# Sums of the modulation pieces on TensorE, placed ahead of the turns of a head's output

## The chip, the cores and the metric

The kernel runs on one core of one Trainium2 chip. The time is the device time of one execution, in microseconds (us); where several executions are given, their median counts.

## What is computed

A trunk of two layers, 1024 tokens by 1024 features, in f32. Layer 0 mixes by attention, layer 1 by gated linear attention; each is followed by a SwiGLU FFN. Every sub-layer is shifted, scaled and gated by a conditioning vector `c`, and that *modulation* is what the change is about. Cut to what matters:

```python
def reference(x, c, ada_w, ada_b, ...):
    for l in range(DEPTH):
        mod = (jax.nn.silu(c) @ ada_w[l] + ada_b[l])[:, None, :]
        sh1, sc1, g1, sh2, sc2, g2 = jnp.split(mod, 6, axis=-1)
        h = rmsnorm(x, norm_g[l, 0]) * (1 + sc1) + sh1
        ...   # mixer: layer 0 has 4 differential heads (A) and 8 dilated heads (B)
        x = x + (1 + g1) * rmsnorm(y, norm_g[l, 1])
        h = rmsnorm(x, norm_g[l, 2]) * (1 + sc2) + sh2
        y = swiglu(h, ffn_w_gate[l], ffn_w_up[l], ffn_w_down[l])
        x = x + (1 + g2) * rmsnorm(y, norm_g[l, 3])
    return x
```

## The kernel before

TensorE (PE) carries the matmuls, and its instructions run in the order in which they are written. Layer 0's attention is a loop over eight blocks, `attention_block(kind, b, slot, last)`. Blocks 0 to 3 are the four A heads (kind 0), blocks 4 to 7 are four pairs of B heads (kind 1). Within a block PE goes over eight rows n of 128 queries:

- `scores(n, b, slot)` (line 936) multiplies queries by keys; VectorE (DVE) adds the bias and takes the maximum (line 2094), which also frees the score banks. `scores(n + 1)` may start only when row n has been read.
- `turn_weights(n)` (line 957) transposes the softmax weights, and `weigh(n)` (line 970) multiplies them by V.
- `chunk(c)` (lines 822, 823 and 826) is a piece of the next block's input projection: 24 matmuls of 512 columns.

At the end of block b stands a seam, which is where the change is. PE runs `turn_v(b + 1)` (line 922, the next block's V), `scores(0, b + 1)`, and then `turn_out()` (line 982): eight transposes of the block's output `o_sb`, four into bank 4 and four into bank 5. They wait for the output: in kind 0 for DVE's scaling of `o_sb` (line 2153, signalled by the drain at 2155), in kind 1 for ScalarE's (ACT) last copy into it (line 1500). The banks must be free too: DVE copies the next V out of bank 5 at line 2071. After the turns ACT reads each bank into `y_st_hi` (line 1543), DVE subtracts that to get `y_st_lo` (line 2163 in kind 0, 2166 in kind 1), and only then does DVE go on to the next block's row 0 (line 2094), which `scores(1)` of the next block waits for.

The modulation is worked out in pieces beside this. In block b (0 to 6) DVE adds up eight weight rows times `silu(c)` into `acc_one` (part of `rinv`, lines 2052 and 2054). `ada_sum(b)` (lines 906 to 913) then sums over the 128 partitions on PE, with two matmuls by a tile of ones into banks 1 and 3. The trace shows each f32 matmul as two records, so there are four records at line 912. DVE's `columns` (line 2003) reads the result in row 1 of the next block; `scores(4)` waits for that through `mod_done`. `ada_sum(b)` is called after `attention_block` returns, so it stands behind the turns.

Below, seam b is the stretch from `scores(0, b + 1)` to the first chunk of block b + 1. Seam 6 has no chunk behind it.

Of the kernel before, what the change touches and what calls it, by code (L numbers as in the profile page):

```python
# [51 lines left out]
def trunk_kernel(nc, xT, cT, weights, ada_w, ada_bT, norm_gT, lam_p, subln_g, w_g2, b_g2, head_g,  # L52
# [5 lines left out]
    with ctx:  # L58
# [47 lines left out]
        def bank(b, n=512):  # L106
            return ps[:, b * 512:b * 512 + n]
# [260 lines left out]
        def lanes(kind, n):  # L368

            if kind == 0:  # L370
                if n < 4:
                    return [(0, n % 2, 0, n + 1)]
                return [(0, 0, 0, 4), (0, 1, 4, n - 3)]
            out = []
            for k0 in range(0, n + 1, 4):
                for c in (0, 1):
                    out.append((c, c, k0, min(4, n + 1 - k0)))
            return out

        def lane_count(kind, n, lane):  # L380

            return 1 + sum(g[1] == lane for m in range(n) for g in lanes(kind, m))

        def events(b, t):
            return LANE[0] * min(b, 4) + LANE[1] * max(b - 4, 0) + t
# [419 lines left out]
        def _(pe):  # L805
# [23 lines left out]
            def chunk(c):  # L829

                u, half = chunk_of(c)
                if c > 1:
                    before = c - 2 if c < 7 else c - 1
                    if before % 6 < 4:
                        pe.wait_ge(qk_lo, qk_count(before))
                    else:
                        pe.wait_ge(v_out, v_count(before))
                unit(u, u % 2, chunk_bank(c), half if c in (0, 2) else None, hh[half], hl[half], done=ch_done)
# [67 lines left out]
            def ada_sum(b):  # L906

                pe.wait_ge(acc_done, b + 2)
                pe.wait_ge(s_read[0], 8 * b + 9)
                pe.wait_ge(s_read[1], 8 * b + 9)  # L910
                for i in range(2):
                    mm = pe.matmul(bank(1 + 2 * i), ones[:, :], acc_one[:, i * 512:(i + 1) * 512], start=True, stop=True)
                mm.then_inc(ada_mm, 1)

            def turn_v(b, group):
                pe.wait_ge(v_out, 2 * b + 2)
                for lane in range(2):

                    pe.wait_ge((ta_free, td_free)[lane], group)
                    for n in range(4):  # L920
                        m = 4 * lane + n
                        mm = pe.transpose(bank(4 + lane)[:, n * P:(n + 1) * P], v_sb[:, m * P:(m + 1) * P], ident[:, :])
                    mm.then_inc((ta_done, td_done)[lane], 1)

            def scores(n, b, slot):
                pe.wait_ge(s_read[0], 8 * b + n + 1)
                pe.wait_ge(s_read[1], 8 * b + n + 1)
                if n == 0:
                    pe.wait_ge(qk_lo, 4 * b + 4)
                W = 256 * ((n + 2) // 2)  # L930
                for k0 in range(0, W, 512):
                    w = min(512, W - k0)
                    for term, (q, k) in enumerate(((q_high, k_high), (q_low, k_high), (q_high, k_low))):
                        for c in range(2):
                            rows = slice(64 * c, 64 * c + 64)
                            mm = pe.matmul(ps[:, c * 1024 + k0:c * 1024 + k0 + w],  # L936
                                           q[slot][rows, n * P:(n + 1) * P], k[slot][rows, k0:k0 + w],
                                           start=term == 0, stop=term == 2)
                            if term == 2 and k0 + w == W:
                                mm.then_inc(s_done[c], 1)  # L940

            def attention_block(kind, b, slot, last=False):
                before = lambda t: events(b, t)

                def turn_weights(n, part=0):

                    count = [lane_count(kind, n, lane) + part for lane in range(2)]
                    if kind == 0:
                        pe.wait_ge(w_done, 8 * b + n + 1 + 1)
                    for c, lane, k0, m in lanes(kind, n):  # L950
                        if kind == 1 and k0 != 4 * part:
                            continue
                        if kind == 1:
                            pe.wait_ge(exp_done, 16 * b + 2 * n + c + 1 + 1)
                        pe.wait_ge((ta_free, td_free)[lane], before(count[lane]) + 1)
                        for i in range(m):
                            mm = pe.transpose(bank(4 + lane)[:, i * P:(i + 1) * P],  # L957
                                              pr[n % 2][:, c, (k0 + i) * P:(k0 + i + 1) * P], ident[:, :])
                        mm.then_inc((ta_done, td_done)[lane], 1)
                        count[lane] += 1  # L960

                def weigh(n):

                    pe.wait_ge(ta_free, before(lane_count(kind, n + 1, 0)) + 1)
                    pe.wait_ge(td_free, before(lane_count(kind, n + 1, 1)) + 1)
                    pe.wait_ge(o_done, 8 * b + n + 1)
                    for c in range(1 if kind == 0 else 2):
                        for kb in range(n + 1):

                            mm = pe.matmul(bank(6)[:, c * P:(c + 1) * P], wT[n % 2][c][:, kb, :],  # L970
                                           v_tok[:, kb, :], start=kb == 0, stop=kb == n)
                    mm.then_inc(pv_done, 1)

                def turn_out():
                    if kind == 0:
                        pe.wait_ge(o_ready, b + 1)
                    else:
                        pe.wait_ge(o_done, 8 * b + 8 + 1)
                    for lane in range(2):
                        pe.wait_ge((ta_free, td_free)[lane], before(LANE[kind] + (not last)))  # L980
                        for n in range(4):
                            mm = pe.transpose(bank(4 + lane)[:, n * P:(n + 1) * P], o_sb[:, 4 * lane + n, :], ident[:, :])
                        mm.then_inc((ta_done, td_done)[lane], 1)

                scores(1, b, slot)
                for n in range(8):
                    if kind == 1:
                        turn_weights(n)
                        if n:
                            weigh(n - 1)  # L990
                    if n == 2 and b:
                        pe.wait_ge(mod_done, b + 1)
                    if n < 6:
                        scores(n + 2, b, slot)
                    if kind == 0:
                        turn_weights(n)
                        if n:
                            weigh(n - 1)
                    elif n > 3:
                        turn_weights(n, 1)  # L1000
                    if n < 6 and not last:
                        chunk(6 * (b + 1) + n)
                        if (b, n) == (6, 5):
                            pe.drain().then_inc(unit_used, 24)
                weigh(7)
                if not last:
                    turn_v(b + 1, before(LANE[kind]))
                    scores(0, b + 1, 1 - slot)
                turn_out()

            def attention():

                for c in range(6):
                    chunk(c)
                turn_v(0, 1)
                scores(0, 0, 0)
                for b in range(HEADS):
                    attention_block(b // 4, b, b % 2, b == HEADS - 1)
                    if b < 7:
                        ada_sum(b)  # L1020
                pe.wait_ge(ta_free, 4 * sum(LANE) + 1)
                pe.wait_ge(td_free, 4 * sum(LANE) + 1)

# [1432 lines left out]
```

## Time and profile before

| | |
|---|---|
| time, median of 3 executions | 2680.44 us (2679.87 to 2685.88) |
| time of the profiled execution | 2687.1 us |
| its span | 2685.2 us |
| PE busy | 2541.0 us, 95% of the span |
| DVE, ACT, POOL busy | 51%, 40%, 43% |
| the 28 records of line 912 | 592 ns at the least, 593 ns median, 1062 ns at the most |
| the 64 records of line 982 | 272 ns at the least, 273 ns median, 477 ns at the most |

A row of a timeline gives the start in us from the span's start, the time from the first start to the last end, the engine, the line, the operation with its output and inputs, the count, and in brackets how long the engine had been idle before it and who ended that. Matmuls overlap, so the time of one record is more than its distance to the next.

### The profile page before, as it was taken

Reading aid. Unit: us, or ns where it says so; the run is one execution under the profiler, and the core shown is the slowest. Engines: PE = TensorE matmul, PEld = TensorE weight load, DVE = VectorE, ACT = ScalarE, POOL = GpSimd, SP = SyncE. Lnnn points to the kernel's source line nnn. Section 1 sums busy time; section 2 is a strip of 40 time slices with the busy share of each in tenths; the row PEclk is TensorE's granted clock in tenths of the full one; section 3 lists DMA queues with packets and bytes.
Section 4 is the critical chain, followed back from the end, with each engine's and each line's share of the span. In section 5 each row is a group of like instructions: output and inputs, shape, how many; then the busy total and the mean of one; then the engine's idle time right before and its main releaser. Section 6 shows DMA issues by size and latency. Waiting matters only on the chain.

```text
span 2685.2 us, 33902 instructions
## 1 busy us (share of the span) xinstructions
PE 2541.0 (95%) x12152; PEld 2073.0 (77%) x12152; DVE 1356.1 (51%) x1877; ACT 1078.5 (40%) x1837; POOL 1147.7 (43%) x648
## 2 busy tenths in 40 slices
PE   5999999998999999999999999997999999999996
PEld 3777777777778888788887777886878888788885
DVE  7466665442464333455356536667366332355145
ACT  3344543343454332334233236656454333234222
POOL 0111111011656777444444434443556777544443
PEclk8999999999999999999999999999999999999998
DMA  6233332224233122342434741223223221343333
GB/s 262 64 106 106 111 103 86 89 92 174 93 108 106 67 91 79 133 141 94 160 122 171 264 146 65 68 71 117 86 99 114 79 91 67 106 142 119 111 133 109
DMA packets 106886, 305.14 MB, mean 114 GB/s; under 512 B 11456, under 2 KB 11776, under 8 KB 106752
## 3 DMA queue, kind: packets, MB, share of 16 engines
q1 hardware_dynamic: 106752, 303.40, 32.9%
q8 instruction: 79, 1.29, 0.2%
q14 instruction: 55, 0.45, 0.1%
HBM read 262.46 MB, written 40.89 MB: 113 GB/s over the span
## 4 chain that ended last, share of the span: by engine, by line
PE 61%; issue 17%; POOL 7%; DVE 6%; ACT 3%; DVEq 2%; DMA 2%; POOLq 2%; SPq 1%; ACTq 0%
PE ps L822 8%; PE ps L826 8%; PE ps L823 8%; PE ps L1190 5%; PE ps L1186 5%; PE ps L1187 5%; POOL w_lo L696 5%; PE ps L970 3%; PE ps L1217 3%; PE ps L1220 3%; PE ps L1214 3%; PE ps L936 2%; PE ps L1039 2%; PE ps L957 2%; DVEq L2223 2%
## 5 line engine op out<-in xcount | busy, mean ns | idle before, releaser
L696 POOL TENSOR_TENSOR w_lo<-w_raw,w_hi 128x1024 fp32r<-128x1024 f32 x258 | 632.0, 2452 | 1344.3 <-ACT w_hi L1285 585.4
L822 PE MATMUL ps<-h_hi,w_hi 128*128 128x512 f32 x1288 | 521.7, 405 | 21.4 <-DVE h_lo L1827 8.4
L823 PE MATMUL ps<-h_lo,w_hi 128*128 128x512 f32 x1288 | 510.2, 396 | 0.0
L1285 ACT ACTIVATE w_hi<-w_raw 128x1024 fp32r<-128x1024 f32 x178 | 188.3, 1058 | 448.5 <-PE ps L1220 293.6
L826 PE MATMUL ps<-h_hi,w_lo 128*128 128x512 f32 x1288 | 319.6, 390 | 0.0
L1895 DVE TENSOR_TENSOR a_lo<-arena,a_hi 128x512 fp32r<-128x512 f32 x88 | 206.8, 2350 | 221.7 <-ACT a_hi L1752 221.7
L822 PEld LDWEIGHTS ps<-h_hi,w_hi 128*128 128x128 f32 x1288 | 246.8, 192 | 89.6 <-DVE h_lo L1827 15.1
L823 PEld LDWEIGHTS ps<-h_lo,w_hi 128*128 128x128 f32 x1288 | 247.1, 192 | 52.1 <-issue 2.4
L826 PEld LDWEIGHTS ps<-h_hi,w_lo 128*128 128x128 f32 x1288 | 243.1, 189 | 50.9
L1186 PE MATMUL ps<-comb,w_hi 128*128 128x512 f32 x560 | 217.8, 389 | 0.0
L1187 PE MATMUL ps<-comb,w_hi 128*128 128x512 f32 x560 | 217.8, 389 | 0.0
L745 POOL TENSOR_TENSOR w_lo<-a_f,w_hi 128x512 fp32r<-128x512 f32 x112 | 144.5, 1293 | 79.0 <-ACT w_hi L1379 79.0
L1214 PE MATMUL ps<-a_hi,w_hi 128*128 128x512 f32 x672 | 168.3, 391 | 7.9 <-issue 6.8
L1217 PE MATMUL ps<-a_lo,w_hi 128*128 128x512 f32 x672 | 168.5, 393 | 0.0
L1220 PE MATMUL ps<-a_hi,w_lo 128*128 128x512 f32 x672 | 166.7, 390 | 0.0
L1379 ACT ACTIVATE w_hi<-a_f 128x512 fp32r<-128x512 f32 x112 | 70.8, 632 | 230.3 <-PE ps L1190 83.2
L1214 PEld LDWEIGHTS ps<-a_hi,w_hi 128*128 128x128 f32 x672 | 126.0, 188 | 36.6 <-issue 8.5
L1190 PE MATMUL ps<-comb,w_lo 128*128 128x512 f32 x560 | 149.7, 389 | 0.0
L1217 PEld LDWEIGHTS ps<-a_lo,w_hi 128*128 128x128 f32 x672 | 128.1, 191 | 26.8
L1220 PEld LDWEIGHTS ps<-a_hi,w_lo 128*128 128x128 f32 x672 | 126.8, 189 | 26.5
L1485 ACT ACTIVATE pr_flat<-pr_flat,small 128x256 f32<-128x256 f32 (+7 forms) x128 | 98.3, 769 | 108.3 <-DVE small L2099 108.3
L1190 PEld LDWEIGHTS ps<-comb,w_lo 128*128 128x128 f32 x560 | 105.1, 188 | 21.8
(263 smaller groups left out, 4230.2 us busy)
## 6 DMA issues: line engine op xcount, KB each, us to landing
w_raw<-weights SPq DMA_DIRECT2D x286, 512.0 KB, 3.6
arena<-ada_w SPq DMA_DIRECT2D x80, 512.0 KB, 3.6
arena<-act_d SPq DMA_DIRECT2D x72, 256.0 KB, 3.7
act_d<-ybuf SPq DMA_DIRECT2D x56, 256.0 KB, 2.2
arena<-ada_w SPq DMA_DIRECT2D x8, 1024.0 KB, 14.8
x<-xT SPq DMA_DIRECT2D x4, 2048.0 KB, 13.3
glr<-weights SPq DMA_DIRECT2D x14, 512.0 KB, 3.6
rinv<-weights SPq DMA_DIRECT2D x28, 256.0 KB, 4.2
```

The costliest lines, as they stand in the source:

```text
L696: pool.tensor_tensor(w_lo[:, s, :], w_raw[:, s, :], w_hi[:, s, :].bitcast(f32), ALU.subtract).then_inc(lo_done, 1)
L822: pe.matmul(bank(b), w, high[:, k, :], start=k == 0, stop=False)
L823: pe.matmul(bank(b), w, low[:, k, :], start=False, stop=False)
L826: mm = pe.matmul(bank(b), w_lo[:, s, k * P:(k + 1) * P], high[:, k, :], start=False, stop=k == KB - 1)
L1186: pe.matmul(bank(b), w, high[:, k, :], start=k == 0, stop=False)
L1187: pe.matmul(bank(b), w, low[:, k, :], start=False, stop=False)
L1190: mm = pe.matmul(bank(b), combo_part(w_lo, q)[:, k * P:(k + 1) * P], high[:, k, :], start=False, stop=k == KB // 2 - 1)
L1214: pe.matmul(bank(m), w_hi[:, slot, cols[m]], a_hi[:, s, :], start=first, stop=False)
L1217: pe.matmul(bank(m), w_hi[:, slot, cols[m]], a_lo[:, s, :], start=False, stop=False)
L1220: mm = pe.matmul(bank(m), w_lo[:, slot, cols[m]], a_hi[:, s, :], start=False, stop=False)
L1285: a.activation(w_hi[:, slot, :], w_raw[:, slot, :], ACT.Copy).then_inc(hi_done, 1)
L1895: v.tensor_tensor(a_lo[:, u % 2, :], act_source(half, u), a_hi[:, u % 2, :].bitcast(f32), ALU.subtract)\
```

## The change

`ada_sum(b)` moves from behind the block to ahead of `turn_out()`. Its two matmuls and its three waits are the same.

```diff
@@ attention_block
                 if not last:
                     turn_v(b + 1, before(LANE[kind]))
                     scores(0, b + 1, 1 - slot)
+                if b < 7:
+                    ada_sum(b)
                 turn_out()
@@ attention
                 for b in range(HEADS):
                     attention_block(b // 4, b, b % 2, b == HEADS - 1)
-                    if b < 7:
-                        ada_sum(b)
                 pe.wait_ge(ta_free, 4 * sum(LANE) + 1)
```

PE at seam 0, where the turns wait for DVE. `arena` is V on its way to being turned, `qk_flat` the queries and keys, `rinv` holds the sums, and `glr` is `o_sb`. A count covers matmuls, not records:

```order
 L922 MATMUL ps<-ident,arena 128x128 x8
 L936 MATMUL ps<-qk_flat_61 128x256 x6
+L912 MATMUL ps<-rinv,ones 128x512 x2
 L982 MATMUL ps<-ident,glr 128x128 x8
-L912 MATMUL ps<-rinv,ones 128x512 x2
 L936 MATMUL ps<-qk_flat_61 128x256 x6
 L936 MATMUL ps<-qk_flat_61 128x512 x6
```

The two sums went from behind the eight turns to ahead of them, directly after the next block's row 0 scores.

PE at seam 5, between two kind 1 blocks. `pr_flat` holds the softmax weights:

```order
 L922 MATMUL ps<-ident,arena 128x128 x8
 L936 MATMUL ps<-qk_flat_60 128x256 x6
+L912 MATMUL ps<-rinv,ones 128x512 x2
 L982 MATMUL ps<-ident,glr 128x128 x8
-L912 MATMUL ps<-rinv,ones 128x512 x2
 L936 MATMUL ps<-qk_flat_60 128x256 x6
 L957 MATMUL ps<-ident,pr_flat 128x128 x2
```

The same exchange; the row 1 scores now follow the turns directly. All seven seams change alike, and the orders of DVE, ACT, POOL and SP stay as they are.

## Rows read from the trace of the kernel before

**Rows 1.** The page, busy time: us, share of the span, instructions of each engine.
```profile
PE 2541.0 (95%) x12152; PEld 2073.0 (77%) x12152; DVE 1356.1 (51%) x1877; ACT 1078.5 (40%) x1837; POOL 1147.7 (43%) x648
```

**Rows 2.** PE's longest waits, 100 to 360 us, then 360 to 600 us.
```profile
PE ps L982 <- DVEq L2155: 6.7, 4, 2.0
...
PE ps L957 <- ACT wt_flat L1479: 5.4, 7, 1.2
```

**Rows 3.** Timeline of PE at seam 0.
```profile
158.07 0.61 PE L936 MATMUL ps<-qk_flat 64*128 64x256 f32 x6
160.27 0.66 PE L982 MATMUL ps<-ident,glr 128*128 128x128 f32 x4 [1.58 <-DVEq L2155]
161.12 0.66 PE L982 MATMUL ps<-ident,glr 128*128 128x128 f32 x4 [0.19 <-DVE arena L2071]
161.61 3.56 PE L912 MATMUL ps<-rinv,ones 128*128 128x512 f32 x4
165.11 0.62 PE L936 MATMUL ps<-qk_flat 64*128 64x256 f32 x6
```

**Rows 4.** Timeline of DVE at seam 0.
```profile
163.80 0.29 DVE L2094 CUSTOM_DVE_ANT_0 pr_flat<-ps,arena 128x128 f32<-128x128 f32 x1
```

**Rows 5.** Timeline of PE at seam 2.
```profile
292.29 0.66 PE L982 MATMUL ps<-ident,glr 128*128 128x128 f32 x4 [1.58 <-DVEq L2155]
...
296.27 0.62 PE L936 MATMUL ps<-qk_flat 64*128 64x256 f32 x6 [0.75 <-DVE small L2094]
297.97 1.47 PE L936 MATMUL ps<-qk_flat 64*128 64x512 f32 x6 [1.08 <-DVE small L2094]
...
299.50 0.78 PE L822 MATMUL ps<-h_hi,w_hi 128*128 128x512 f32 x1
...
301.71 0.39 PE L823 MATMUL ps<-h_lo,w_hi 128*128 128x512 f32 x1
```

**Rows 6.** Timeline of PE at seam 1, then at seam 3.
```profile
226.67 1.97 PE L982 MATMUL ps<-ident,glr 128*128 128x128 f32 x8 [1.95 <-DVEq L2155]
...
231.11 0.62 PE L936 MATMUL ps<-qk_flat 64*128 64x256 f32 x6
...
358.86 0.66 PE L982 MATMUL ps<-ident,glr 128*128 128x128 f32 x4 [1.59 <-DVEq L2155]
...
363.64 0.63 PE L936 MATMUL ps<-qk_flat 64*128 64x256 f32 x6
```

**Rows 7.** Timeline of PE at seam 5.
```profile
512.73 0.62 PE L936 MATMUL ps<-qk_flat 64*128 64x256 f32 x6
513.28 1.09 PE L982 MATMUL ps<-ident,glr 128*128 128x128 f32 x8
514.20 1.88 PE L912 MATMUL ps<-rinv,ones 128*128 128x512 f32 x4
516.91 0.62 PE L936 MATMUL ps<-qk_flat 64*128 64x256 f32 x6 [0.82 <-DVE small L2094]
...
519.50 0.50 PE L822 MATMUL ps<-h_hi,w_hi 128*128 128x512 f32 x1
...
521.92 0.39 PE L822 MATMUL ps<-h_hi,w_hi 128*128 128x512 f32 x1
```

**Rows 8.** Timeline of PE at seam 4: a chunk's first and eleventh matmul.
```profile
441.31 0.61 PE L822 MATMUL ps<-h_hi,w_hi 128*128 128x512 f32 x1
...
445.28 0.39 PE L822 MATMUL ps<-h_hi,w_hi 128*128 128x512 f32 x1
```

**Rows 9.** Stretches at seams 0, 2, 5, 6; us, busy us (records) by engine, granted clock, DMA, GB/s.
```profile
161.67:165.08 3.41, 3.41 (x5) 0.91 (x4) 2.21 (x7) 2.64 (x5) 0.00 (x0) 0.50 0.27 107
298.20:301.61 3.41, 3.41 (x12) 2.33 (x11) 2.65 (x10) 1.54 (x6) 0.00 (x0) 0.50 1.00 338
...
513.00:522.00 9.00, 7.75 (x43) 4.97 (x42) 6.62 (x29) 4.09 (x15) 0.00 (x0) 1.00 0.57 199
595.16:601.99 6.83, 6.33 (x28) 5.21 (x28) 5.96 (x32) 3.25 (x13) 0.00 (x0) 0.50 0.73 241
```

## The prediction, made before the changed kernel was run

> **What bounds the kernel now.** I read the page's busy times first. TensorE is busy for 95% of the span [rows 1], so the time changes only where something on TensorE's own path changes. The waits of TensorE in the attention stage come next. Its longest is the one that the change aims at: the turns of an A head's output wait for DVE's scaling, 6.7 us over four seams [rows 2]. In the second stretch the longest wait is for ACT, and no wait for a DMA comes before it in that list. So a seam that ends later is not caught up by a transfer that was late anyway: I take a delay of the seam as a delay of the kernel.
>
> Then I read the seams one by one. Three things are to be seen.
>
> (a) The sums take little when the clock is full. At seam 5 the four records take 1.88 us from first start to last end and one takes 0.59 us (the least in the table above), so they start (1.88 - 0.59) / 3 = 0.43 us apart and hold TensorE for 4 x 0.43 = 1.72 us [rows 7].
>
> (b) Behind the turns a second gap opens, and the sums stand in it. After the turns ACT and DVE must read both banks, and DVE must read row 0 of the next block, before the next scores may start. At seam 5 the sums ran in that gap and TensorE still sat idle for 0.82 us [rows 7]; at seam 2 it sat idle for 0.75 us [rows 5]. There the sums cost nothing today.
>
> (c) The granted clock drops to 0.50, the 1.2 GHz level, for stretches of 3.41 us near the seams, after TensorE has had pauses, and what lies in such a stretch takes twice as long. At seam 0 it fell on the sums: 3.56 us [rows 3, 9]. At seam 2 it fell on the scores and on the first matmuls of the chunk [rows 5, 9]. At seam 5 there was none from 513 to 522 us [rows 9]. At seam 6 it was 6.83 us long [rows 9].
>
> **The change, part by part.**
>
> *Seams 0 to 3 at full clock: nothing.* The scores of row 0 start at 158.07 and hold TensorE for 0.55 us (512.73 to 513.28 with no idle time between [rows 7]). The sums then run from 158.62 to 160.34, and the first turns start 0.07 us later than today's 160.27 [rows 3]. The second four turns wait for DVE's copy until 161.12 in either order [rows 3], and it is these that the path goes through. The wait of 1.6 us is filled, but what was taken out behind the turns was hidden, so the next scores start when DVE has read row 0, as they do at seam 2. Sum: 0.
>
> *Seams 4 to 6 at full clock: a loss.* At seam 5 the turns follow the scores with no wait [rows 7]. Put ahead of them, the sums hold them back by the whole 1.72 us. Behind the turns are queued ACT's reads, DVE's low parts, row 0 on DVE and then the next scores; all of that was waited for today, as the idle 0.82 us before 516.91 shows [rows 7], and all of it moves by 1.72 us. The cover that hid the sums is left empty. Three seams: 3 x 1.72 = **+5.2 us**. This is the firmest term; only 1.72 us per seam is in play, so its bounds are 0 (some slack later in the block takes it) and 5.2.
>
> *The clock: what the low stretches cost today.* From the first turns to the next scores took 296.27 - 292.29 = 3.98 us at seam 2, at full clock [rows 5]. It took 4.84 us at seam 0 [rows 3], 4.44 at seam 1 and 4.78 at seam 3 [rows 6], so the low clock cost 0.86, 0.46 and 0.80 there. At seam 0 this agrees with DVE: its second read of row 0 starts at 163.80 [rows 4], and at seam 2 the scores start 0.45 us after that read, so here they could have started at 164.25 and not at 165.11. At seam 2 it cost 0.5 us on the scores (1.47 against about 0.95 us at full clock) and about 1.0 on the chunk: five distances between matmuls took 301.71 - 299.50 = 2.21 us [rows 5] against 5 x 0.24 = 1.21 at seam 5, where ten took 521.92 - 519.50 = 2.42 [rows 7]. Sum over seams 0 to 3: 0.86 + 0.46 + 1.5 + 0.80 = 3.6 us. At seam 4 ten distances took 3.97 us [rows 8] against 2.42, so a whole stretch on a chunk costs 1.55 us. Seam 5: none.
>
> *The clock: what they will cost.* The order of today puts 1.72 us of dense matmuls between two pauses, and at seams 0, 1 and 3 they caught much of the slow time where it is half hidden. In the new order there is one long pause from the end of the turns (161.8 at seam 0) to the scores at 164.25, then 0.6 us of work and another pause of some 1.1 us: over 4 us with little in it. I expect a low stretch behind it at every seam, on scores and chunk, where nothing hides it. One stretch costs 1.55 us there. Two in a row, as at seam 6, where waits break up the work of the first, would cost 3.1. I take the middle, 2.3, since the scores of the next rows still have waits between them when the stretch begins. Seams 0 to 3: 4 x 2.3 - 3.6 = +5.6 us (between +2.6 and +8.8). Seams 4 and 5: 2 x 2.3 - 1.55 = +3.1 us (+1.55 to +4.65). Seam 6 has two today: 0. Sum for the clock: **+8.7 us**, between +4.2 and +13.5.
>
> A rule speaks against the change too. The Trainium skill, "TensorE: Matmul & The Clock Gate", section "HAM oscillation — how this bites in real kernels", says that pauses between bursts of matmuls let the gate fall back to the slow level, so that each burst begins slow, and calls for an order of work that keeps them together. By that rule the sum is that of the clock term, about +14; without it +5.2. The trace agrees in kind: six of the seven seams show slow work, seam 5 does not.
>
> *The rest.* The three waits of the sums are met before they come: the pieces are summed by DVE in row 7, ahead of the copies that the last product needs, and the score banks were already waited for by the scores just ahead. The readers of the sums come a row later, so nobody gains by having them 2 us earlier. No other engine's order moves.
>
> *Against the profiled execution:* 2687.1 + 5.2 + 8.7 = 2701.0 us. That execution stands 6.7 us above the median of 2680.44, so on the scale of the median it is 2680.4 + 13.9 = **2694 us**.
>
> **The rivals.**
>
> *A: only the shift.* The low stretches are as many and as costly as today, and the delay at seams 4 to 6 is all: +5.2 us, 2685.6. For it: their place in the seams is different each time (on sums, on turns, on the chunk), so a new order may just deal them anew. Against it: the longer pause.
>
> *B: the sums keep the clock up, and the kernel is not slower.* In seams 0 to 3 the sums now run in the wait of 1.6 to 1.95 us ahead of the turns, so that TensorE works on without a break until the turns are done. If that pause is what sets off the low stretches, they go: 3.6 us at seams 0 to 3, 1.55 at seam 4, about 3.1 at seam 6, together -8.3, against +5.2: -3.1 us, 2677.3. It decides in favour of the change once more than 5.2 us of slow time are saved. For it: at seams 0, 1 and 3 the clock fell during or just after that wait. Against it: the gap behind the turns grows by as much as the one ahead shrinks, and seams 4 and 6 fell slow with no wait ahead of the turns.
>
> *C: nothing is passed on.* The 1.72 us at seams 4 to 6 vanish in the later rows, where TensorE waits for ACT anyway, and the clock deals as today: 0, 2680.4. Against it: ACT and DVE begin the block later by the same 1.72 us, so those waits move with it.
>
> **How the numbers follow.** About 0.3%, 8.0 us, is what a measurement of this kernel can tell from no change. Chances: forecast 0.62, A 0.27, B 0.06, C 0.05. The forecast's case runs from 5.2 + 4.2 = +9.4 to 5.2 + 13.5 = +18.7, all slower by over 0.3%; A reaches over that line now and then through a stretch dealt otherwise. Slower 0.65, same 0.33, faster 0.02. The range runs from 2684, inside A, to 2700, above the forecast's upper end of 2699.1; it leaves out B, C and the low half of A.
>
> **What would show it.** At seams 4 to 6 the turns start 1.72 us behind where they start now (513.28 + 1.72 at seam 5) and TensorE's idle time before the next scores grows from 0.8 to about 2.5 us. At seams 0 to 3 the wait of the turns for DVE falls from 1.6 us to about nothing, and an idle time of about 2.4 us appears before the next scores. The granted clock is 0.50 behind most seams, on chunk matmuls 0.43 us apart. I am wrong on the clock if the low stretches stay few, and wrong on the shift if the turns at seam 5 start where they did or if the block behind them is shorter by as much.

## The result: slower by half a per cent

| | before | changed |
|---|---|---|
| time, median | 2680.44 us (5 executions) | 2695.75 us (5 executions, 2693.41 to 2697.67) |
| ratio of the times | | 1.0053, 95% interval 1.0041 to 1.0066 |
| time of the profiled execution | 2687.1 us | 2696.83 us |
| its span | 2685.2 us | 2694.9 us |

The change costs 15.3 us by the medians and 14.2 us by the ratio, whose interval runs from 11.0 to 17.7. The forecast was 2694 us.

### The profile page after: what moved, and what is told of

It reads as the page before. It is cut to its first block, busy times and chain, and to the rows that moved or that the text cites. A ratio compares the mean times of both kernels' runs of the same rounds, so it can differ in the third digit from the quotient of the medians.

```text
span 2694.9 us, 33902 instructions
## 1 busy us (share of the span) xinstructions
PE 2542.1 (94%) x12152; PEld 2074.8 (77%) x12152; DVE 1355.2 (50%) x1877; ACT 1078.6 (40%) x1837; POOL 1148.1 (43%) x648
## 4 chain that ended last, share of the span: by engine, by line
PE 61%; issue 17%; POOL 7%; DVE 5%; ACT 3%; DVEq 2%; DMA 2%; POOLq 2%; SPq 1%; ACTq 0%
PE ps L822 8%; PE ps L826 8%; PE ps L823 8%; PE ps L1187 5%; PE ps L1190 5%; PE ps L1186 5%; POOL w_lo L696 5%; PE ps L970 3%; PE ps L1217 3%; PE ps L1220 3%; PE ps L1214 3%; PE ps L936 3%; PE ps L1039 2%; PE ps L957 2%; DVEq L2223 1%
## 5 line engine op out<-in xcount | busy, mean ns | idle before, releaser
L1187 PEld LDWEIGHTS ps<-comb,w_hi 128*128 128x128 f32 x560 | 105.1, 188 | 21.8
## 6 DMA issues: line engine op xcount, KB each, us to landing
arena<-ada_w SPq DMA_DIRECT2D x8, 1024.0 KB, 14.9
x<-xT SPq DMA_DIRECT2D x4, 2048.0 KB, 13.3
```

The source lines that it names most:

```text
L1187: pe.matmul(bank(b), w, low[:, k, :], start=False, stop=False)
```

## The profile after

The page's busy times hardly move, as the work is the same. (The columns are those of [rows 1].)

```profile
PE 2542.1 (94%) x12152; PEld 2074.8 (77%) x12152; DVE 1355.2 (50%) x1877; ACT 1078.6 (40%) x1837; POOL 1148.1 (43%) x648
```

PE's waits for DVE's reading of row 0 in the kernel before, first from 100 to 360 us and then from 360 to 600 us (us in total, times, longest):

```profile
PE ps L936 <- DVE small L2094: 4.0, 4, 1.1
...
PE ps L936 <- DVE small L2094: 3.8, 7, 0.8
```

PE's waits in the changed kernel, in the same two stretches:

```profile
PE ps L936 <- DVE small L2094: 10.6, 6, 2.5
...
PE ps L982 <- DVE arena L2071: 0.2, 1, 0.2
...
PE ps L936 <- DVE small L2094: 8.1, 5, 2.5
```

The wait that the change aimed at is gone: the 6.7 us of the turns for DVE's scaling [rows 2] have no row any more. In its place the scores wait for DVE's reading of row 0, up to 2.5 us at a time: 10.6 us where it was 4.0. In the second stretch, where no wait was removed, it is 8.1 us where it was 3.8.

The timeline of PE at seam 0 after the change shows both, and what the clock makes of it:

```profile
155.60 0.62 PE L936 MATMUL ps<-qk_flat 64*128 64x256 f32 x6
156.15 1.98 PE L912 MATMUL ps<-rinv,ones 128*128 128x512 f32 x4
157.97 1.34 PE L982 MATMUL ps<-ident,glr 128*128 128x128 f32 x8
161.79 1.01 PE L936 MATMUL ps<-qk_flat 64*128 64x256 f32 x6 [2.48 <-DVE small L2094]
163.88 1.65 PE L936 MATMUL ps<-qk_flat 64*128 64x512 f32 x6 [1.08 <-DVE small L2094]
...
172.54 0.97 PE L936 MATMUL ps<-qk_flat 64*128 64x512 f32 x6
```

It answers to [rows 3]. The sums take 1.98 us and not 3.56, the turns follow without a wait, and then PE is idle for 2.48 us. The next two groups of scores are slow (1.01 and 1.65 us, against 0.62 and 0.98 at full clock). From `scores(0)` to `scores(3)` of the next block is 16.94 us. In the kernel before it was 173.55 - 158.07 = 15.48 us, by its `scores(3)`:

```profile
173.55 0.96 PE L936 MATMUL ps<-qk_flat 64*128 64x512 f32 x6
```

Some of the stretches of low clock behind the seams of the changed kernel, at seams 0, 1, 3 and 5 (columns as in [rows 9]):

```profile
161.50:168.30 6.80, 5.43 (x20) 3.90 (x21) 4.51 (x21) 3.10 (x12) 0.00 (x0) 0.50 0.90 295
229.80:236.60 6.80, 5.75 (x21) 4.10 (x21) 4.82 (x22) 3.55 (x13) 0.00 (x0) 0.50 0.89 293
...
366.30:369.70 3.40, 3.40 (x11) 2.14 (x11) 2.48 (x11) 1.26 (x5) 0.00 (x0) 0.51 1.01 324
...
523.30:526.70 3.40, 3.40 (x11) 2.33 (x12) 2.72 (x13) 1.63 (x6) 0.00 (x0) 0.51 0.98 312
```

There is one behind each of the seams 0 to 5: 6.8 us long behind seams 0 to 2, 3.4 us behind seams 3 to 5. All of them lie on scores and chunk.

At seam 5 the shift can be read from the chain of work that ended last, which is followed back from the end of the stretch. This is a piece of it, before the change (start in us, us, what):

```profile
512.80 0.55 PE ps L936 x6
513.35 0.60 PE ps L982 x4
```

and after:

```profile
515.67 0.56 PE ps L936 x6
516.22 1.91 PE ps L912 x4
518.14 0.45 PE ps L982 x4
```

The sums were not on the chain and now they are.

From such rows comes a table of the seams. Each number is the time from `scores(0)` to `scores(3)` of the next block, in us, in one profiled execution. "Full clock" is what a seam took where the granted clock stayed at 1.00 and no added work held up its end. For seams 0 to 3 it comes from a run with the sums in both places (below); at seam 3 one run had the old order at full clock as well, and took 15.3 us too. For seams 4 and 5 it is the old order in the first experiment, and at seam 5 in the kernel before.

| seam | 0 | 1 | 2 | 3 | 4 | 5 |
|---|---|---|---|---|---|---|
| full clock | 14.6 | 15.0 | 14.6 | 15.3 | 13.3 | 13.3 |
| before | 15.5 | 15.4 | 16.0 | 16.2 | 14.9 | 13.3 |
| changed | 16.9 | 17.4 | 17.2 | 16.7 | 16.6 | 16.6 |

Seams 0 to 3 grew by 5.1 us in sum and seams 4 and 5 by 5.0. Seam 6 grew by 1.7 (9.3 to 11.0). The rows between the seams are as long as before to 0.03 us (50.55 us in blocks 1 to 3), but for one low stretch in block 5 of the kernel before (506.4 to 509.8 us), which this execution of the changed kernel does not have, and for the rows behind seam 6, which took 1.2 us more (20.1 against 18.9) with a low stretch on them. Over the attention stage, from `scores(0)` at seam 0 to 616.40 us before and 625.55 us after, that makes 11.6 us.

## The experiments

Three theories stood against each other. Theory 1 is that of the prediction: a shift at seams 4 to 6, and low stretches of the clock brought by the emptied gap behind the turns. Theory 2 is rival A, the shift alone. Theory 3 stands for the other rivals as each expectation puts it. The kernel before was timed again beside them. For the first three below and for the idle work at seams 0 to 3 its median is 2682.47 us (29 executions); for the other three it is 2681.66 us (23 executions). A difference "by the ratio" is the ratio times that median. Added lines shift the line numbers: line 936 (scores) becomes 937 or 941, line 982 (turns) 983 or 987, line 912 (sums) 917 in some, line 2094 (DVE's reading) 2096 to 2103, and line 2155 (its drain) 2164.

### The new order at seams 0 to 3 only

```diff
+                if b < 4:
+                    ada_sum(b)
                 turn_out()
+                if 4 <= b < 7:
+                    ada_sum(b)
```

> The sums ahead of the turns at seams 0 to 3 only; behind them, as before, at seams 4 to 6. Theory 1 (shift and clock): nothing at full clock, because the wait for DVE hides the sums, but low stretches move to scores and chunk: +5.6 us on the kernel before (+2.6 to +8.8), and the rows show about 2.4 us idle before the next scores. Theory 2 (shift only, low stretches dealt as before): within 1 us of the kernel before. Theory 3 (the filled wait keeps the clock up): -3.6 us.

Measured: 2687.86 us, ratio 1.0019 (1.0010 to 1.0028), +5.1 us by the ratio (2.7 to 7.5) where theory 1 said +5.6. PE at seam 0:

```profile
158.55 1.34 PE L982 MATMUL ps<-ident,glr 128*128 128x128 f32 x8
162.37 0.68 PE L936 MATMUL ps<-qk_flat 64*128 64x256 f32 x6 [2.47 <-DVE small L2096]
164.10 1.65 PE L936 MATMUL ps<-qk_flat 64*128 64x512 f32 x6 [1.05 <-DVE small L2096]
```

The wait ahead of the turns is gone and the kernel is slower. At these seams nothing is shifted: the scores of row 1 start 3.82 us after the turns, which is the 3.98 us of full clock at seam 2 before [rows 5] less the turns' own wait for the bank (0.19 us). What is lost is lost behind them, at low clock. Theories 2 and 3 fall for seams 0 to 3.

### The new order at seams 4 to 6 only

```diff
+                if 4 <= b < 7:
+                    ada_sum(b)
                 turn_out()
+                if b < 4:
+                    ada_sum(b)
```

> The sums ahead of the turns at seams 4 to 6 only; behind them at seams 0 to 3. Theory 1: the shift of 1.8 us at each of three seams, +5.5 us, and low stretches on the chunks at seams 4 and 5, +3.1 us: +8.6 us on the kernel before. Theory 2: +5.5 us. Theory 3 (absorbed later in the block): 0.

Measured: 2691.56 us, ratio 1.0036 (1.0022 to 1.0050), +9.7 us by the ratio (5.9 to 13.4). Theory 1 had said +8.6; theory 2's +5.5 lies just below the interval. The two halves add up: 5.1 + 9.7 = 14.8 us against 14.2 for the whole by the ratio and 15.3 by the medians. PE at seam 4, and the granted clock over seam 3 (old order), in seam 4 and in seam 5 (columns as in [rows 9]):

```profile
440.68 0.62 PE L936 MATMUL ps<-qk_flat 64*128 64x256 f32 x6 [2.54 <-DVE small L2096]
...
442.38 1.65 PE L936 MATMUL ps<-qk_flat 64*128 64x512 f32 x6 [0.29 <-DVE small L2096]
...
352.00:374.00 22.00, 17.77 (x109) 13.21 (x108) 15.42 (x51) 11.19 (x31) 2.24 (x1) 1.00 0.34 121
442.00:448.80 6.80, 6.51 (x18) 4.69 (x18) 4.86 (x29) 2.56 (x9) 0.00 (x0) 0.50 0.68 227
523.90:527.30 3.40, 3.40 (x11) 2.33 (x12) 2.71 (x15) 1.66 (x6) 0.00 (x0) 0.50 0.98 300
```

Here seam 4 has two low stretches in a row and takes 18.1 us, where the changed kernel had one and took 16.6. Seams 4 and 5 together grew by 6.5 us: twice 1.8 for the shift, and 2.9 for the clock.

### The sums twice, ahead of the turns and behind them

```diff
+                if b < 7:
+                    ada_sum(b, False)   # same sums, nobody is told
                 turn_out()
+                if b < 7:
+                    ada_sum(b)
```

> The changed kernel, with the same two sums worked out a second time behind the turns at all seven seams (added work: 14 matmuls, about 12 us of TensorE time, all of it meant to lie in the gap behind the turns). Theory 1: the long pause behind the turns was what brought the low stretches, so they go or shrink and this kernel, though it does more, is faster than the changed kernel by 5 to 10 us: +5 to +10 us on the kernel before rather than +15. Theory 2: the low stretches have nothing to do with the pause; it is as slow as the changed kernel or slower, +15 us or more.

Measured: 2685.37 us, ratio 1.0010 (1.0001 to 1.0019), +2.7 us (0.3 to 5.1). With 14 more matmuls it is some 12 us faster than the changed kernel, more than the 5 to 10 us that theory 1 had expected. Theory 2 falls here. No low stretch is left at seams 0 to 5; one stands between them, in block 5. At seam 5 the shift then stands alone:

```profile
507.90 0.62 PE L937 MATMUL ps<-qk_flat 64*128 64x256 f32 x6
508.45 1.98 PE L912 MATMUL ps<-rinv,ones 128*128 128x512 f32 x4
510.28 1.04 PE L983 MATMUL ps<-ident,glr 128*128 128x128 f32 x8
511.15 1.88 PE L912 MATMUL ps<-rinv,ones 128*128 128x512 f32 x4
513.86 0.62 PE L937 MATMUL ps<-qk_flat 64*128 64x256 f32 x6 [0.82 <-DVE small L2097]
...
523.02 0.96 PE L937 MATMUL ps<-qk_flat 64*128 64x512 f32 x6
```

The seam takes 523.02 - 507.90 = 15.12 us against 13.34 before (526.07 - 512.73), so the shift is 1.8 us. The second copy of the sums sits in the gap and costs nothing: the scores still wait 0.82 us, exactly as in [rows 7].

### The sums twice at seams 0 to 3, behind only at 4 to 6

```diff
+                if b < 4:
+                    ada_sum(b, False)
                 turn_out()
+                if b < 7:
+                    ada_sum(b)
```

> At seams 0 to 3 the sums ahead of the turns and worked out again behind them; at seams 4 to 6 behind only, as before. Theory 1: no shift (the turns wait for DVE anyway), and no low stretch at seams 0 to 3: -2 to -3.6 us on the kernel before; the run with the sums twice at all seams differs from this one by the shift alone, 5.5 us. Theory 2 (the clock has nothing to do with it): 0 to +1 us.

This is the first experiment plus one thing, the sums repeated behind the turns at seams 0 to 3. PE at seam 0, and below it the whole stretch of that seam with the granted clock:

```profile
158.75 1.34 PE L983 MATMUL ps<-ident,glr 128*128 128x128 f32 x8
159.93 1.88 PE L912 MATMUL ps<-rinv,ones 128*128 128x512 f32 x4
162.56 0.63 PE L937 MATMUL ps<-qk_flat 64*128 64x256 f32 x6 [0.76 <-DVE small L2097]
164.26 0.96 PE L937 MATMUL ps<-qk_flat 64*128 64x512 f32 x6 [1.07 <-DVE small L2097]
...
157.00:174.00 17.00, 15.08 (x70) 9.89 (x71) 12.80 (x48) 7.74 (x21) 0.00 (x0) 1.00 0.37 125
162.30:169.10 6.80, 5.46 (x30) 4.20 (x31) 5.21 (x27) 3.56 (x13) 0.00 (x0) 1.00 0.90 301
```

The clock stays at 1.00, and it does so with the DMA engines busy for 0.90 of the time (301 GB/s), as they were in the low stretch at this seam of the changed kernel (0.90, 295 GB/s): the DMA traffic is not what lowers the clock. The scores take 0.96 us where they took 1.65, and the seam takes 14.6 us where the first experiment's took 17.1. Seams 0 to 3 add up to 59.5 us, against 63.1 before and 68.8 in the first experiment. In the trace that is the gain of 3.6 us which theory 1 gave as its upper end. The whole kernel measured 2680.19 us, ratio 0.9994 (0.9984 to 1.0005): an interval from -4.3 to +1.3 us, which does not tell -2 us from 0. The profiled execution (2672.58 us) was one of the fastest of the twelve. But the interval lies wholly below that of the first experiment (1.0010 to 1.0028), which does less work: filling the gap behind the turns made the kernel faster.

### Idle work in the pauses of the old order, seams 0 to 3

The filler is one 512-column f32 matmul of a constant tile into bank 7, which is free there.

```diff
+            def filler(n):
+                for i in range(n):
+                    pe.matmul(bank(7), ones[:, :], dist[:, 0:512], start=True, stop=True)
...
                 scores(1, b, slot)
+                if 0 < b < 5:
+                    filler(1)
...
+                if b < 4:
+                    filler(1)
                 turn_out()
+                if b < 7:
+                    ada_sum(b)
```

> The kernel before with idle work added at seams 0 to 3, its result used by nobody: one 512-column f32 matmul in the wait ahead of the turns, and one in the pause between the scores of rows 1 and 2. Theory 1: the pauses bring the low stretches, worth 3.6 us at seams 0 to 3; with shorter pauses some or all of them go: -1 to -3.6 us. Theory 2: no effect of the pauses: 0 to +1 us, for what the added matmuls hold up.

Measured: 2677.27 us, ratio 0.9979 (0.9969 to 0.9990), -5.6 us by the ratio (-8.3 to -2.7), and so faster than the kernel before with work added that nobody uses. PE at seam 0:

```profile
158.01 1.12 PE L909 MATMUL ps<-arena,ones 128*128 128x512 f32 x2
159.66 0.66 PE L987 MATMUL ps<-ident,glr 128*128 128x128 f32 x4 [0.53 <-DVEq L2164]
...
161.00 1.88 PE L917 MATMUL ps<-rinv,ones 128*128 128x512 f32 x4
163.64 0.62 PE L941 MATMUL ps<-qk_flat 64*128 64x256 f32 x6 [0.76 <-DVE small L2103]
164.19 1.12 PE L909 MATMUL ps<-arena,ones 128*128 128x512 f32 x2
165.34 0.96 PE L941 MATMUL ps<-qk_flat 64*128 64x512 f32 x6
```

The wait of 1.58 us [rows 3] is 0.53 and the pause of 1.1 us is filled. The granted clock is 1.00 from 150 to 580 us, over seams 0 to 5:

```profile
150.00:420.00 270.00, 254.10 (x1476) 199.60 (x1477) 177.64 (x424) 133.96 (x314) 32.80 (x13) 1.00 0.32 104
420.00:580.00 160.00, 150.16 (x969) 125.87 (x968) 80.81 (x196) 62.29 (x148) 18.02 (x7) 1.00 0.25 80
```

The middle of the interval is larger than the 3.6 us expected at most, but 3.6 lies inside it. In the trace seams 4 and 5 and block 5 ran without a low stretch too, though nothing was changed there. That is not the fillers' doing alone: in the first experiment and in the one above, which have the old order at seams 4 and 5, those seams ran at full clock as well. It is the low stretches of the kernel before at seam 4 and in block 5 that are not always there.

### A longer block of idle work ahead of the turns at seams 4 to 6

```diff
+                if 4 <= b < 7:
+                    filler(4)
                 turn_out()
+                if b < 7:
+                    ada_sum(b)
```

> The kernel before, with four 512-column f32 matmuls that nobody uses ahead of the turns at seams 4 to 6 (twice the length of the sums); the sums stay behind the turns. It measures the shift with the gap behind the turns still covered. Theory 1: 8 records 0.43 us apart and 0.1 us for the first, 3.5 us at each of three seams, all passed on to the end: +10.6 us, less up to 1.6 us if the low stretch at seam 4 goes. Theory 3 (absorbed later in the block): 0 to +3 us.

Measured: 2690.39 us, ratio 1.0035 (1.0022 to 1.0048), +9.4 us by the ratio (5.9 to 12.9). PE at seam 5:

```profile
512.15 0.63 PE L941 MATMUL ps<-qk_flat 64*128 64x256 f32 x6
512.71 3.70 PE L909 MATMUL ps<-arena,ones 128*128 128x512 f32 x8
516.24 1.04 PE L987 MATMUL ps<-ident,glr 128*128 128x128 f32 x8
...
519.83 0.62 PE L941 MATMUL ps<-qk_flat 64*128 64x256 f32 x6 [0.83 <-DVE small L2101]
...
528.98 0.96 PE L941 MATMUL ps<-qk_flat 64*128 64x512 f32 x6
```

The seam takes 528.98 - 512.15 = 16.83 us, 3.5 more than before, for 3.53 us of work ahead of the turns (512.71 to 516.24). Twice the work gives twice the shift (1.8 for the sums). Three times 3.53 is 10.6 us, inside the interval, and the mean granted clock is the same 0.982 as in the kernel before. That refutes rival C. The trace agrees: the rest of the block behind seam 5 takes 62.1 us, as it does in the kernel before, so nothing is taken up there.

### Idle work in more of the pauses

`filler` has a second argument here, the number of columns.

```diff
                 scores(1, b, slot)
+                if 0 < b < 5:
+                    filler(1)
...
+                if b < 4:
+                    filler(1)
+                    filler(1, 256)
                 turn_out()
+                if b < 7:
+                    ada_sum(b)
+                    filler(1, 256)
```

> The kernel before, with idle work in more of the pauses: at seams 0 to 3 one and a half 512-column matmuls ahead of the turns and one between the scores of rows 1 and 2, at all seams half a one behind the sums. Theory 1: no low stretch at seams 0 to 3 and fewer at 4 to 6: -4 to -7 us on the kernel before, at least as good as the run with fillers at seams 0 to 3 (-5.6 us), less some 0.1 us at a seam where the added work overfills its gap. Theory 2: slower than before by what the added work holds up, +1 us.

Measured: 2676.62 us, ratio 0.9987 (0.9978 to 0.9996), -3.5 us by the ratio and -5.0 by the medians. It is faster than the kernel before (-5.9 to -1.1 us), but the middle falls short of the -4 to -7 us that theory 1 had given, and it is not faster than the run with fewer fillers. At seams 0 to 5 that one already had no low stretch, so there was little left to win.

## Why the prediction was right

*Seams 0 to 3 at full clock: 0.* Right. With the clock at 1.00 and the sums in both places, seam 0 takes 14.6 us, as it does with the sums behind and fillers in the pauses; seam 3 takes 15.3 us with the sums in both places and 15.3 in the old order. Filling the wait of 6.7 us [rows 2] won nothing, because what left the second gap had been hidden there.

*Seams 4 to 6: 3 x 1.72 = +5.2.* Right in mechanism, a little small: 1.8 us each, +5.4. The longest record of the sums in the trace takes 697 ns where the least takes 592, and at seam 5 they hold PE from 516.15 to 517.97, 0.1 us more than the forecast's 1.72.

*What the low stretches cost in the kernel before: 3.6 at seams 0 to 3, 1.55 at seam 4.* Right for the execution that it was read from: 63.1 - 59.5 = 3.6 and 14.9 - 13.3 = 1.6, against seams with no low stretch. The one at seam 4 was not typical. In three other traces with nothing changed at seams 4 and 5 (the first experiment, the sums twice at seams 0 to 3, idle work at seams 0 to 3) neither seam has one.

*What they cost now: 2.3 us per seam.* Right on average for seams 0 to 3, where it was 2.3, 2.5, 2.6 and 1.4 us, and +5.1 against +5.6 in the sum. That the middle between one and two stretches fitted was luck: there were two in a row at three seams and one at the fourth. At seams 4 and 5 it was too high in this execution. One stretch each, 1.5 us, makes +1.4 and not +3.1. In the second experiment, with the same order there, seam 4 had two and the two seams cost +2.9. What decides between one and two is not shown. The forecast put the clock at nothing at seam 6, where with the rows behind it it cost some 1.2 us, and it left out the low stretch in block 5, whose absence gave 1.5 us back.

*The sum.* In the traces the attention stage grew by 11.6 us: 5.4 by the shift, 6.2 by the clock, where the forecast had 5.2 + 8.7 = 13.9. The executions differ by 14.2 us (ratio) or 15.3 (medians). The trace of the kernel before shows too small a difference, because the execution that was profiled took long: it stood 6.7 us above the median, with a granted clock of 0.979. The mean granted clock over all executions shows this:

| kernel | executions | mean granted clock | us at the low level |
|---|---|---|---|
| before | 29 and 23 | 0.9817 and 0.9820 | 98 and 97 |
| changed | 5 | 0.9786 | 115 |
| new order at seams 0 to 3 | 12 | 0.9798 | 108 |
| new order at seams 4 to 6 | 6 | 0.9800 | 108 |
| sums twice, all seams | 11 | 0.9832 | 90 |
| sums twice, seams 0 to 3 | 12 | 0.9840 | 86 |
| idle work, seams 0 to 3 | 12 | 0.9848 | 82 |
| longer block ahead, seams 4 to 6 | 5 | 0.9820 | 97 |
| idle work in more pauses | 11 | 0.9851 | 80 |

The last column is an estimate, 2 x (1 - clock) x span, which takes 0.50 as the only low level. The changed kernel spends 17 to 18 us more at the low level by it; in the two traces the difference is 10 us. At 1.5 us lost in 3.4 us of it on dense work that is up to 8 us (an estimate), and with the shift 5.4 + 8 = 13.4 us. That is close to the 14.2 measured. That the forecast came within 2 us of 2695.75 is still partly luck: a clock term that was 2.5 us too high for the profiled pair met a profiled execution that took longer than most.

*The rivals.* A (shift only) falls by the first and third experiments. B (the sums keep the clock up) had the right observation, that pauses bring the low stretches, and overlooked that the one behind the turns grew by what the one ahead lost. Counted over all nine traces, seams 0 to 3 had a low stretch in 11 of 12 cases with the old order and nothing added there, in 8 of 8 with the new order (6 times two in a row), and in 0 of 16 with work both ahead of the turns and behind them. Seams 4 and 5, where no wait stands ahead of the turns, had one in 1 of 14 cases with work behind the turns and in 4 of 4 with none. How short each pause must be is not shown: the pause of 1.1 us between the scores of rows 1 and 2 stayed open in the runs with the sums twice, and the clock stayed at 1.00. C falls by the longer block of idle work. As for the Trainium skill, "TensorE: Matmul & The Clock Gate", section "HAM oscillation — how this bites in real kernels", which the prediction cites, the traces agree in kind: breaking up the dense work cost clock, and filling the pauses gave it back. The section's example has waits of 3 to 5 us for a DMA; here a pause of 2.5 us, 0.6 us of scores and a pause of 1.1 us (0.3 at seam 5) were enough.

## What to carry to other kernels

Before moving work into a wait, look at the gap that it leaves: work that is hidden in its present place gives nothing when it is moved, and it delays everything behind it wherever the new place has no wait. On TensorE the pauses had a second price in this kernel: the clock fell to 0.50 behind them and slowed whatever came next, 1.5 us for a low stretch on a chunk. So weigh a move by the pauses that it leaves as well as by the wait that it removes. Where a pause can't be removed, useless matmuls that fit into it can pay (5.6 us here), and a shift is measured cleanly only when the clock has been held equal on both sides.

## What was not expected of the hardware

Work whose result nobody uses made the kernel 5.6 us faster (ratio 0.9969 to 0.9990), with one 512-column f32 matmul in each of two pauses at four seams. Repeating the sums behind the turns changed a seam from 17.1 to 14.6 us. The low stretches between 150 and 650 us were 3.4 us long or 6.8 in all nine traces. And the time at the low level goes with the spread of the executions: 29 of the kernel before, on one chip, ran from 2675.42 to 2687.68 us, the two with a granted clock of 0.985 at 2675.6 us on average and the 14 with 0.981 at 2683.5.
